# Tokens in four transfers instead of one, turned quarter by quarter, and the small rows through GpSimd's queue

## What is computed

```python
def rms_norm(x, w):
    xf = x.astype(jnp.float32)
    y = xf * lax.rsqrt(jnp.mean(xf * xf, axis=-1, keepdims=True) + NORM_EPS)
    return (y * w.astype(jnp.float32)).astype(x.dtype)

def diff_attention(h, w_in, q_gain, k_gain, lam_params, subln_w, w_out, rel_bias, lambda_init):
    q, k, v = jnp.split(h @ w_in, 3, axis=-1)
    q = rms_norm(q.reshape(b, s, ATTN_HEADS, 2, d), q_gain).transpose(3, 0, 2, 1, 4)
    k = rms_norm(k.reshape(b, s, ATTN_HEADS, 2, d), k_gain).transpose(3, 0, 2, 1, 4)
    ...

def reference(x, ...):
    for i in range(DEPTH):
        h = rms_norm(x, norm_mix[i])
        if i % 2 == 0:
            x = x + diff_attention(h, attn_w_in[j], ...)
            h = rms_norm(x, norm_ffn[i])
            x = x + swiglu(h, ffn_w_gate[j], ffn_w_up[j], ffn_w_down[j])
        else:
            x = x + ssd_mixer(h, ssd_w_in[j], ...)
            h = rms_norm(x, norm_ffn[i])
            x = x + moe_swiglu(h, moe_router[j], ...)
    return x
```

## Time and profile before

| | us |
|---|---|
| three timed runs | 1568.09, 1568.57, 1569.09 (median 1568.57) |
| profiled execution, its time | 1568.66 |
| its span | 1566.9 |
| TensorE busy | 1545.3 |
| VectorE busy | 1303.5 |
| ScalarE busy | 1100.2 |

### The profile page before, as it was taken

The page is one execution under the profiler, slowest core; times in us unless marked ns, Lnnn a source line. Parts: engine busy times, 40 slices in busy tenths (PEclk is TensorE's granted clock), DMA queues, the critical chain, the costliest instruction groups (busy, mean ns, idle before and its releaser), DMA issues.

```text
span 1566.9 us, 24788 instructions
## 1 busy us (share of the span) xinstructions
PE 1545.3 (99%) x9121; PEld 1348.4 (86%) x9121; DVE 1303.5 (83%) x1589; ACT 1100.2 (70%) x1295; POOL 67.9 (4%) x57
## 2 busy tenths in 40 slices
PE   9999999999999999999999999999999999999997
PEld 7879999999999998888888888888888888888886
DVE  6766655555799877999999999999999999999996
ACT  5676444444566656788888878888888888788785
POOL 0001100100001000000000000000000000000000
PEclk9999999999999999999999999999999999999999
DMA  9335445445343359999999999999999999999980
GB/s 345 111 135 185 171 164 207 168 168 175 142 162 108 109 211 396 378 390 379 393 385 358 394 385 353 393 388 353 393 388 350 394 390 350 394 388 352 394 325 12
DMA packets 188260, 455.72 MB, mean 291 GB/s; under 512 B 4089, under 2 KB 4587, under 8 KB 188187
## 3 DMA queue, kind: packets, MB, share of 16 engines
q1 hardware_dynamic: 185082, 444.48, 76.9%
q0 software_dynamic: 2928, 10.17, 2.5%
q10 hardware_dynamic: 176, 0.07, 0.0%
HBM read 449.45 MB, written 5.26 MB: 290 GB/s over the span
## 4 chain that ended last, share of the span: by engine, by line
issue 56%; PE 36%; DVE 4%; POOL 2%; ACT 1%; DMA 1%; POOLq 0%; ACTq 0%; DVEq 0%
PE bank L683 36%; DVE split_mem L1622 1%; POOL mem L657 1%; POOL out L649 1%; DMA h_rows<-mem 1%; DVE mem L1809 1%; DVE mem L1777 0%; DVE mem L1821 0%; ACT split_mem L1173 0%; DMA rows<-norm_mix 0%; DVE mem L1648 0%; DVE split_mem L2184 0%; DVE mem L1579 0%; DVE split_mem L1600 0%; DVE mem L1589 0%
## 5 line engine op out<-in xcount | busy, mean ns | idle before, releaser
L683 PE MATMUL bank<-split_mem 128*128 128x256 f32 (+1 forms) x8064 | 1442.4, 339 | 3.9 <-DVE split_mem L2184 1.3
L683 PEld LDWEIGHTS bank<-split_mem 128*128 128x128 f32 x8064 | 1243.7, 190 | 171.1 <-issue 6.5
L2184 DVE TENSOR_TENSOR split_mem<-mem,split_mem 128x1024 fp32r<-128x1024 f32 x668 | 806.6, 1223 | 66.0 <-ACT split_mem L1507 24.6
L1507 ACT CAST split_mem<-mem 128x1024 fp32r<-128x1024 f32 x672 | 707.1, 1054 | 188.2 <-PE bank L683 187.2
L1622 DVE TENSOR_TENSOR split_mem<-mem,split_mem 128x1024 fp32r<-128x1024 f32 x172 | 213.3, 1254 | 118.7 <-ACT split_mem L1173 118.6
L1173 ACT CAST split_mem<-mem 128x1024 fp32r<-128x1024 f32 x172 | 177.6, 1044 | 133.2 <-PE bank L683 129.8
L683 PE MATMUL bank<-mem 128*64 128x128 f32 (+6 forms) x382 | 45.3, 309 | 3.7 <-DVE mem L1556 1.5
L683 PEld LDWEIGHTS bank<-mem 128*64 128x64 f32 (+2 forms) x382 | 33.7, 165 | 10.5 <-issue 7.1
L1514 ACT ACTIVATE mem<-bank,small 96x512 f32<-96x512 f32 x56 | 38.4, 685 | 2.1 <-DVE small L2129 2.1
L2191 DVE TENSOR_TENSOR mem<-mem,bank 96x512 f32<-96x512 f32 x56 | 37.9, 676 | 0.0
L1777 DVE SCALAR_TENSOR_TENSOR mem<-mem,colA 128x253 f32<-128x253 f32 (+2 forms) x72 | 31.5, 479 | 4.0 <-ACT mem L1257 3.1
(11 more groups left out here) (203 smaller groups left out, 509.2 us busy)
## 6 DMA issues: line engine op xcount, KB each, us to landing
mem<-moe_w_gate SPq DMA_DIRECT2D x56, 2048.0 KB, 9.3
mem<-moe_w_up SPq DMA_DIRECT2D x56, 2048.0 KB, 9.9
mem<-moe_w_down SPq DMA_DIRECT2D x56, 2048.0 KB, 9.9
mem<-ssd_w_in SPq DMA_DIRECT2D x10, 2048.0 KB, 7.9
mem<-ffn_w_gate SPq DMA_DIRECT2D x7, 2048.0 KB, 8.3
mem<-ffn_w_up SPq DMA_DIRECT2D x7, 2048.0 KB, 7.9
mem<-ffn_w_down SPq DMA_DIRECT2D x7, 2048.0 KB, 7.9
mem<-attn_w_in SPq DMA_DIRECT2D x5, 2048.0 KB, 11.2
```

The lines of the kernel that those rows point to most:

```text
L683: return nc.tensor.matmul(o, lhsT, rhs, start=start, stop=stop, skip_group_check=shared)
L1507: nc.scalar.copy(wsplit[:, EXPERT_BUFFER[n % SPLITS], 0, :].rearrange("p (k n) -> p k n", n=w.shape[2]), quarter(w, q)).then_inc(w_hi, 1)
L2184: tt_(lo, quarter(w, q), hi.bitcast(F32), ALU.subtract).then_inc(w_lo, 1)
```

## The change

- The tokens are fetched by four transfers of 256 of the 1024 columns, each with a semaphore of its own, and each is issued ahead of a quarter of tile q. `const` comes after the last quarter.
- `norm_mix` and the thirteen small transfers are issued by GpSimd, `norm_mix` first.
- TensorE turns a quarter of the tokens (`turn_x`) at a time: quarters 0 and 1 ahead of q0, quarter 2 ahead of q1, quarter 3 ahead of q2. VectorE takes them one at a time too.
- `ROWS_AT` moves from 1 to 3, `MEAN_AT` from 3 to 4. VectorE's `bias_and_skip_tables` moves behind `raw_lo(0, 3)`.
- One product on ones is left of three at the start, and the three products of 512 columns ahead of q0 become six of 128 columns.

```diff
-ROWS_AT, MEAN_AT = 1, 3
+ROWS_AT, MEAN_AT = 3, 4
...
         @block.sync
         def _(sp):
-            sp.dma_start(xin[:, :, :], x[0].rearrange("(a p) n -> p a n", p=P)).then_inc(in_x, 16)
             for q in range(4):
+                sp.dma_start(xin[:, :, 2 * P * q:2 * P * (q + 1)],
+                             x[0].rearrange("(a p) n -> p a n", p=P)[:, :, 2 * P * q:2 * P * (q + 1)]).then_inc(in_x[q], 16)
                 sp.dma_start(quarter(view("attn_q", DENSE_SLOT[0]), q), quarter(SOURCE["attn_q"](0), q))\
                     .then_inc(in_first[q], 16)
-                if q == 1:
-                    sp.dma_start(cst[:, P:NCONST], const[:, P:NCONST]).then_inc(in_const, 16)
-            for src, part, r0, c0 in (
...
-                sp.dma_start(rows[r0:r0 + n, part, c0:c0 + wd], src).then_inc(in_rows, 16)
-            sp.dma_start(small[0:SH, 16:17], ssd_d[0].rearrange("(n a) -> n a", a=1)).then_inc(in_misc, 16)
-            sp.dma_start(relb[0:BUCKETS, :], rel_bias).then_inc(in_misc, 16)
-            sp.dma_start(onehot[:, :], hot).then_inc(in_misc, 16)
-            sp.dma_start(lam_in, attn_lambda.rearrange("o a d -> o (a d)").broadcast_to([P, 4 * HD])).then_inc(in_lam, 16)
+            sp.dma_start(cst[:, P:NCONST], const[:, P:NCONST]).then_inc(in_const, 16)
...
         @block.gpsimd
         def _(pool):
+
+            pool.dma_start(rows[0:16, 1, :], norm_mix.rearrange("i (b p) -> (i b) p", p=P)).then_inc(in_mix, 16)
+            for src, part, r0, c0 in (
...
+                pool.dma_start(rows[r0:r0 + n, part, c0:c0 + wd], src).then_inc(in_rows, 16)
+            pool.dma_start(small[0:SH, 16:17], ssd_d[0].rearrange("(n a) -> n a", a=1)).then_inc(in_misc, 16)
+            pool.dma_start(relb[0:BUCKETS, :], rel_bias).then_inc(in_misc, 16)
+            pool.dma_start(onehot[:, :], hot).then_inc(in_misc, 16)
+            pool.dma_start(lam_in, attn_lambda.rearrange("o a d -> o (a d)").broadcast_to([P, 4 * HD])).then_inc(in_lam, 16)
...
             pe.wait_ge(ones_set, 1)
-            for _ in range(3):
+            for _ in range(1):
                 mm(bank[3][:, :], ones[:, 0:P], ones[:, 0:512], True, True)
...
-            pe.wait_ge(in_x, 16)
-            for i in range(4):
+            def turn_x(i):
+
                 B.claim(pe, ("x", i))
+                pe.wait_ge(in_x[i], 16)
...
             def project(tile, banks, q, fresh=None):
+                if fresh == 0 and q == 0:
+                    turn_x(0)
+                    keep_busy(banks[0], 6, P, xin[:, 0, :])
+                if fresh == 0 and q < 3:
+                    turn_x(q + 1)
                 if fresh and q == 0:
                     keep_busy(banks[0], 2)
-                if fresh == 0 and q == 0:
-                    keep_busy(banks[0], 3, 512, xin[:, 0, :])
...
             act.dma_start(cst[:, 0:P], const[:, 0:P]).then_inc(in_ident, 16)
-            act.dma_start(rows[0:16, 1, :], norm_mix.rearrange("i (b p) -> (i b) p", p=P)).then_inc(in_mix, 16)
...
             take_x(0)
-            take_x(1)
             raw_lo(0, 0)
             split(0, 0)
-            take_x(2)
-            take_x(3)
+            take_x(1)
             raw_lo(0, 1)
             split(0, 1)
+            take_x(2)
...
                 if n == 0:
-                    bias_and_skip_tables()
+                    take_x(3)
                     raw_lo(0, 2)
...
                 if n == 0:
                     raw_lo(0, 3)
+                    bias_and_skip_tables()
                     sum_squares(0)
```

More of the change, by code:

```diff
@@ L454, in hybrid_trunk @@
         in_hi, in_lo = sem("in_hi"), sem("in_lo")
-        in_x, in_const, in_rows, in_misc, in_lam = (sem(n) for n in ("in_x", "in_const", "in_rows", "in_misc", "in_lam"))
+        in_x = [sem(f"in_x{i}") for i in range(4)]
+        in_const, in_rows, in_misc, in_lam = (sem(n) for n in ("in_const", "in_rows", "in_misc", "in_lam"))
         in_bias, in_scratch, in_dt, in_router = sem("in_bias"), sem("in_scratch"), sem("in_dt"), sem("in_router")
@@ L588, in _ @@
         def _(pool):
+            pool.dma_start(rows[0:16, 1, :], norm_mix.rearrange("i (b p) -> (i b) p", p=P)).then_inc(in_mix, 16)
+            for src, part, r0, c0 in (
+                    (norm_ffn.rearrange("i (b p) -> (i b) p", p=P), 1, NORM_FFN, 0),
+                    (ssd_conv_b[0].rearrange("(b p) -> b p", p=P), 1, CONV_B, 0),
+                    (ssd_norm[0].rearrange("(b p) -> b p", p=P), 1, SSD_NORM, 0),
+                    (attn_subln, 1, SUBLN, 0),
+                    (attn_q_gain, 1, Q_GAIN, 0), (attn_q_gain, 1, Q_GAIN, HD),
+                    (attn_k_gain, 1, K_GAIN, 0), (attn_k_gain, 1, K_GAIN, HD),
+                    (ssd_conv_w[0].rearrange("j (b p) -> (j b) p", p=P), 0, 0, 0)):
+                n, wd = src.shape
+                pool.dma_start(rows[r0:r0 + n, part, c0:c0 + wd], src).then_inc(in_rows, 16)
[3 more added lines that the diff above has]
+            pool.dma_start(lam_in, attn_lambda.rearrange("o a d -> o (a d)").broadcast_to([P, 4 * HD])).then_inc(in_lam, 16)
             B.released(pool, "ubias")
```

8 lines of the change are left out of this document (removed).

## The result

The changed kernel takes 1573.45 us (median of 8 runs, 1572.8 to 1574.9), the kernel before, run beside it, 1568.53 (8 runs, 1568.09 to 1569.6): a ratio of 1.0031, 95% interval 1.0021 to 1.0041, so +4.9 us. It is slower, and by more than the predicted +2.9. The profiled execution took 1573.48 with a span of 1571.6, against 1568.66 and 1566.9: +4.7 us of span. Of these, 0.1 arise ahead of the first products, 3.4 between them and the QK mean, 0.3 in small pieces over the rest, and 0.9 behind the last issue of a transfer.

A forecast was written before the change was run, and what follows sets the result against it. It took TensorE to bound the kernel, busy 1545.3 of 1566.9 us, so only waits at the beginning could move. Start -0.6 and +3.5 up to the QK mean gave +2.9: 1568.57 to 1571.5 us, range 1569.0 to 1574.0.

The forecast's parts named there:

- Start, -0.6 us: At the start: norm_mix through GpSimd lands 4.9 us after 0.75, so q0's products begin 0.6 us earlier, at 10.75.
- F: Point where TensorE's products of tile q begin: 11.36 us before the change, predicted 10.75; places are counted as F+.
- q1 F+4.0, q2 F+9.2, q3 F+13.4: Tile q's second to fourth quarters begin at these times after F, with waits of 0.65 before q1, 1.85 before q2.
- Mean F+16.3, k q1 F+20.5, QK mean F+24.5: Mean of squares, tile k's second quarter and QK mean come then; delays of +1.9, +0.5 and +1.1 us along the way.
- The +3.5 us up to here: At the QK mean, counted from F: F+24.5 against F+21.0 before, so 3.5 us later.
- Clock in q0, taken 0: Less filling at the start could leave q0 at half speed, costing 0 to +2.3 us; the forecast took 0.
- A shift goes on to the end unchanged, nothing binds there: From the QK mean to the end, TensorE's delay carries through unchanged and no transfer binds, adding 0.
- Second tile and small rows hidden: Tile k's CAST, reached at 22.1, needn't wait for its transfer; small rows land by 19.7, needed at 21.9, cover 2.2 us.
- The sum: The start's -0.6 and the +3.5 us at the QK mean make +2.9 us, thus 1571.5 us.
- the sum's own range: Sum with the ends of start (-1.9 to 0) and clock (0 to +2.3): stated +1.6 to +5.2, thus 1570.2 to 1573.8.
- the third (no earlier start): Rival: norm_mix, issued first by GpSimd, lands no earlier than 6.27; +3.5 us, 1572.1 us; chance 0.13.

The follow-up runs named there:

- e6: Changed kernel with three products on ones at the start instead of one; VectorE's work after the beginning stood 4.04 us later than in the kernel before.
- e5: Changed kernel with norm_mix issued by ScalarE again instead of GpSimd; VectorE's work after the beginning 2.20 us later than before, against 3.56 in the changed kernel.
- e2: Changed kernel with the fourth token quarter turned ahead of q1 and copied right behind the third; VectorE's later work 1.87 us behind the kernel before, against 3.56.
- e3: Changed kernel with MEAN_AT back at 3, the mean ahead of q3; VectorE's work after the beginning came 1.07 us earlier than in the changed kernel.
- e4: Changed kernel with the edits of e2 and e3 together; median 1570.81 us against 1569.53 for the kernel before in the same rounds.
- e11: Kernel of e10 with the 13 small rows issued by GpSimd instead of SyncE, norm_mix left on ScalarE; median 1569.55 us against 1567.53.
- e10: Kernel of e9 with four token transfers ahead of all weight quarters, each turn waiting for its own, and two products on ones; median 1567.53 us.
- e8: Kernel before with ROWS_AT 2 and VectorE's table step behind raw_lo(0, 2); 0.49 of the expected 1.3 us gain arrived.
- e9: Kernel of e8 with ScalarE's constant_columns moved ahead of the CAST of tile k; median 1567.27 us, ratio 0.9982 to the kernel before.
- e7: The kernel before, unchanged, timed and profiled a second time; 1568.58 us, ratio 0.9996.
- e12: Changed kernel with the edits of e4 and e5 together; seven of its 11 runs took 1569.0 to 1570.0 us, the profiled one was slowest.
- e1: Kernel before's order of work and three products on ones, with the changed kernel's transfers; median 1571.46 us.

## Why the prediction was right between the start and the QK mean and off at both ends

1. **Start, -0.6 us: failed.** It was +0.08. The step had three parts. GpSimd issues the row at 1.31, not at 0.75: +0.56. It lands 4.54 after, not 4.9: -0.36. And the turn of quarter 0 took 1.06 instead of 0.60: +0.46, because behind one product on ones instead of three TensorE still ran at half speed (e6 has three again, and there the turn takes 0.66 instead of 1.11; the first record of the granted clock, which is one of full speed, stands at 9.66 in the changed kernel and at 4.95 in e6, and the window views print 1.00 for what lies ahead of it, so there the durations have to be read). Together -0.6 + 0.66 = +0.06. The third is the clock, which I had looked for only in q0. I had said that the slow turns would fill TensorE ahead of F, without counting that they stand on the chain themselves. e5 shows what GpSimd's queue cost: 1.35 us, without which q0 stands 1.27 ahead of before. The rule of the Trainium skill (DMA: Bandwidth & Descriptors, Anatomy of one DMA; a fixed 2.0 us and the bytes) would by an estimate have had the row there in 2.0 us. Measured were 4.5, so the page's figure doesn't hold for this place.
2. **q1 F+4.0, q2 F+9.2, q3 F+13.4: right.** Measured F+3.82, F+8.93, F+13.22. The wait ahead of q2 was 1.57 (1.85 predicted), released by `raw_lo`, and e2 shows its cause.
3. **Mean F+16.3, k q1 F+20.5, QK mean F+24.5: right.** Measured F+16.19, F+20.34, F+24.42, released by the engines named. The +3.5 us up to here was +3.40 from F and, with F itself, +3.48. Counted from F, e2 takes 2.1 of it away, e3 1.2, and both together 3.3.
4. **Clock in q0, taken 0: right for q0** (3.11 us for 24 products, 3.10 before), wrong for the turn (step 1). That the price exists is shown by e6: 1.5 us in q0, well within the 0 to 2.3 that the prediction left for it.
5. **A shift goes on to the end unchanged, nothing binds there: failed.** The shift grew from 3.56 to 3.80, and the DRAIN added 1.14, of which the sooner landing gave back 0.21: +1.17 in all, against a predicted 0. No row names what the 0.24 consists of. I had priced the fourteen issues on GpSimd only where they are made (and there they are free: no wait for small rows, and the CAST of tile k didn't wait). Their number comes back at the closing step.
6. **Second tile and small rows hidden: right.** The CAST of tile k didn't wait for its weights, and the rows waited for nothing.

The sum: +2.9 predicted; +0.7 from the start and +1.2 from step 5 make +4.8, and measured were +4.7 in the profile's span and +4.9 in the median. That 1573.45 still lies in the range of 1569.0 to 1574.0 is in part luck: the range reaches so high for a q0 at the low clock, which didn't come, and the end, which did, was in no term of it. (The upper end of the sum's own range is also added up wrongly: a start of 0 and a clock of +2.3 together make +5.8, not +5.2.) The chances stood at 0.42 for slower by more than 0.2%, which happened, and 0.49 for no visible change. Of the rivals, the third (no earlier start) named the right size of the start, for a wrong reason: `norm_mix` did land 0.42 earlier.

**Open.** In e4, e5 and e11 the median stands 0.7 to 1.5 us above the profiled execution, and no profile of a slower run of them was taken. For e4 the mean granted clock of its runs speaks for a low clock. For e5 it doesn't: all its 11 runs have 0.998, and they took 1571.4 to 1574.8; e11 is mixed (eight runs at 0.998 up to 1570.6, three at 0.997 up to 1570.0). Not tried were more filling between turns and q0 in e6, and e10 with its first weight quarter ahead of the third token transfer, which its waits for weights suggest.

## What to carry to other kernels

Ask of every transfer that is moved to another queue not only who waits for it, but what the new engine does ahead of its first issue and behind its last. A turn or a copy that is put "just in time" is not free when an engine runs its queue in order: what stands behind it waits with it, needed or not; look for the instruction that TensorE needs next and see what stands before it in the queue. And read from the trace what released each wait (e8 to e9): to move one wait away is worth only as much as the next one allows, and the next one has a name.

## What the runs showed of the chip

- **GpSimd's closing DRAIN grows with the DMAs that it issued.** 2.112 us in the five profiles in which it issues 25 (before, e7 to e10), 3.172 with 38 (e5, e11, e12) and 3.253 with 39 (after, e1 to e4, e6): some 0.08 us for each (1.06 for 13, 0.081 for the last), the same to the nanosecond in all that share a count. GpSimd's other instructions are the same in all of them.
- **A small transfer can be held up by a large one on another queue.** `norm_mix`, issued by ScalarE at 1.22 in each case, took 5.1 us beside one token transfer of 1024 KB (before, e7 to e9) and 3.3 and 3.0 beside pieces of 256 KB (e5 and e12, e10 and e11). Each time it landed 0.2 us behind the first token transfer (6.28 behind 6.08 before, 4.50 behind 4.31 in e5, 4.25 behind 4.04 in e10). That the size of the neighbour is the cause is inferred: at that time e10 differs from e9 in it and in the order of SyncE's issues.
- **The granted clock falls with waits, and stays low while TensorE is busy again.** It fell at 11.8 in e6 (idle for 2.38 us until 10.93), at 22.6 in e12 (idle from 21.3 to 22.9) and at 17.8 in e1 (idle for 0.99 until 16.85), and stood at 0.50 for 3.4, 6.8 and 3.4 us. The length of the wait alone doesn't decide: the kernel before idles for 0.26 and 0.93 us at its small rows (1.37 in e7), the changed kernel for 1.57 ahead of q2, and none of these three profiles shows a drop.
